# An expert loop placed at a fixed instruction slot, and GpSimd's attention work cut into four pieces a head

## The chip, the cores and the metric

The kernel runs on one core of a Trainium2 chip. The metric is the device time of one execution in microseconds. The engines are TensorE (PE; its weight loads are listed as PEld), VectorE (DVE), ScalarE (ACT), GpSimd (POOL) and SyncE (SP), which issues most DMAs. Each has its own instruction stream; they meet through semaphores.

## The reference

Two layers (DEPTH) over 512 tokens of width 1024, in float32:

```
h = rmsnorm(x);  proj = h @ w_in
ya = chunk attention, 8 heads, key band of 9 chunks of 64, learned relative bias
yb = sliding-window attention, 8 heads on 2 kv heads, window 128, ALiBi and sinks
x += (sigmoid(gate0) * (ya @ w_a) + sigmoid(gate1) * (yb @ w_b)) @ w_out
layer 0:  x += (silu(h @ w_gate) * (h @ w_up)) @ w_down        # dense, 2816 wide
layer 1:  x += sum over top 2 of 8 experts, softmax weight * swiglu_e(h), 1408 wide
out = rmsnorm(x)
```

## The kernel before, in words

All large products are made at float32 accuracy out of fp32r parts: each weight unit (128x1024) is loaded by SP into `raw`, ACT copies its high part (`split_hi`, L642) and the low part is the difference (L929 on DVE, L480 on GpSimd), and PE multiplies hi·hi, hi·lo and lo·hi. Two split buffers and four raw buffers go round.

**Attention of a layer.** There are 16 heads: 0 to 7 belong to the first mixer (chunk attention, bias from `rel_ext`), 8 to 15 to the second (ALiBi). A head has four steps, one for each block of 128 queries, so a layer has 64. PE, ACT and DVE run a loop of ticks written out by hand (L1467, L738, L1022). A step's scores go to PSUM; DVE adds the bias and takes the maximum (L1032, L1040), ACT takes the exponential, DVE takes the reciprocal and multiplies the probabilities by it (L1049, called the normalisation here, which raises `probs_ready`); two ticks after the scores PE transposes them (L1491, with the bias tile's turning at L1447 in a head's first step) and later multiplies by the values. Between these PE works off one gate unit (L1336 to L1338) every four ticks: gate g is used in ticks 4g to 4g+3.

GpSimd's part (L506 to L528): for each head of the first mixer it issues a DMA of bias rows (L512), masks a corner (L515), makes the low part of a gate unit (`gate_lo`, L480: 1024 columns, as soon as ACT's high part is there), and splits a finished head's output into high (`head_split`, L500) and low part (L502) as soon as DVE has raised `y_added`; for heads of the second mixer it makes the ALiBi tile and its sink column (`distance_tile`, L490, L492).

**Experts.** A loop of eight passes, one for each expert, runs on SP, ACT, DVE and PE (`passes`, L853 on ACT, L1252 on DVE, L1639 on PE). A pass has 35 weight units: 24 gate and up units in three chunks (512, 512 and 384 columns), 11 down units. SP loads seven ahead (`m_raw`), ACT and DVE split five ahead (`m_hi` L839, `m_lo` L1238). Each pass begins with five instructions that load the expert's token count and branch: with more than 128 tokens it runs the Then body (two slots, 128 and 64 rows), else the Else body (one slot). At its end ACT copies the result (`y_stage` L892, and L895 with two slots), and the next pass begins with the load of the activation table (L861). A second loop of the same code, for experts with more than 192 tokens, follows and is skipped. With these inputs experts 0, 1, 6 and 7 take the Then body, 2 to 5 the Else body.

Of the kernel before, what the change touches and what calls it, by code (L numbers as in the profile page):

```python
# [5 lines left out]
F32 = mybir.dt.float32  # L6
# [4 lines left out]
ALU = mybir.AluOpType  # L11
# [3 lines left out]
P = 128  # L15
D = 1024
T = 512
DEPTH = 2
# [40 lines left out]
ROUNDS = -(-T // CAP)  # L59
LISTS = ROUNDS * EXPERTS * SLOTS  # L60
PAD_H, PAD_Y = T, 2 * T


def build_kernel(nc, xT, g_mix, w_in, b_gate, rel_ext, sinks, w_a, w_b, w_out, g_ffn, w_gu, w_down, w_router,
                 moe_gu, moe_down, g_ffn_row, g_final_row, out):
    ctx = ExitStack()
    with ctx:
# [242 lines left out]
        def split_of(n, c0, c1):  # L310

            return w_hi[:, n % SPL, c0:c1], w_lo[:, n % SPL, c0:c1]
# [126 lines left out]
        def _(pool):  # L439
# [27 lines left out]
            def double_keys(layer):  # L467
                for u in K_UNITS:
                    pool.wait_ge(drained_dve, layer * N_PROJ + u + 1)
                    for own, hi, lo, other in halves(u):  # L470
                        pool.dma_start(hi[other, :], hi[own, :]).then_inc(k_doubled, 16)
                        pool.dma_start(lo[other, :], lo[own, :]).then_inc(k_doubled, 16)

            def gate_lo(layer, g):

                n = MIX_START[layer] + U_GATE + g + 2
                hi, lo = split_of(n, 0, UNIT)
                pool.wait_ge(hi_ready, n + 1)
                pool.wait_ge(lo_ready, n)
                pool.tensor_tensor(lo, raw[:, n % RAW, :], hi.bitcast(F32), ALU.subtract).then_inc(lo_ready, 1)  # L480
                pool.wait_ge(lo_ready, n + 1)

            def distance_tile(layer, hh):

                H = layer * 2 * HEADS + hh
                head = step(TT * hh)["head"]
                if hh == HEADS:
                    pool.wait_ge(consts, 4)
                pool.wait_ge(nmax_ready, TT * (H - 1))
                pool.tensor_scalar(bias_t[:, H % 2, 2 * P:T], alibi[:], -2.0 ** -(head + 1), None, ALU.mult)  # L490
                pool.wait_ge(bias_ready, H)
                pool.tensor_copy(bias_t[:, H % 2, T:T + 1], sink[:, layer, head:head + 1]).then_inc(bias_ready, 1)  # L492

            def head_split(layer, hh):

                H = layer * 2 * HEADS + hh
                r = step(4 * hh)["rows"]
                y_hi, y_lo = y_tiles(hh)
                pool.wait_ge(y_added, H + 1)
                pool.tensor_copy(y_hi[r:r + HD, :], y_sum[r:r + HD, :]).then_inc(y_hi_ready, 1)  # L500
                pool.wait_ge(y_hi_ready, H + 1)
                pool.tensor_tensor(y_lo[r:r + HD, :], y_sum[r:r + HD, :], y_hi[r:r + HD, :].bitcast(F32),  # L502
                                   ALU.subtract).then_inc(y_lo_ready, 1)
                pool.wait_ge(y_lo_ready, H + 1)

            for i in range(DEPTH * HEADS):  # L506

                if i % HEADS:
                    pool.wait_ge(bias_turned, i)
                else:  # L510
                    pool.wait_ge(rinv_spread, 2 * (i // HEADS) + 1)
                pool.dma_start(bias[:], bass.AP(tensor=rel_ext.tensor, offset=i * 384, ap=[[1, P], [1, 2 * P]])).then_inc(bias_in, 16)  # L512
                pool.wait_ge(bias_in, 16 * (i + 1))

                pool.memset(bias[HD:P, 3 * HD:4 * HD], MASKED).then_inc(bias_masked, 1)  # L515
                if i % HEADS == 0:
                    double_keys(i // HEADS)
                pool.wait_ge(bias_masked, i + 1)
                if i % HEADS >= 2:
                    gate_lo(i // HEADS, i % HEADS - 2)  # L520
                if i % HEADS >= 3:
                    head_split(i // HEADS, i % HEADS - 3)
                if i % HEADS == HEADS - 1:
                    for j in range(HEADS - 2, 2 * HEADS):
                        gate_lo(i // HEADS, j)
                        head_split(i // HEADS, j - 1)
                        if j + 2 < 2 * HEADS:
                            distance_tile(i // HEADS, j + 2)  # L528
            steps = [0]

            def one(ins):
# [103 lines left out]
        def _(act_):  # L635
# [215 lines left out]
            turned_x(0, 1)  # L851

            def passes(first, sections, always_both):  # L853
                with A.Fori(0, sections) as i:
                    def pass_of(slots):

                        def moved(half, of):
                            A.activation(m_other[:, half, 0:of.shape[1]], of, ACT.Copy).then_inc(tail_moved, 1)


                        A.activation(warm[:], eps[:], ACT.Silu)  # L861
                        for u in range(M_UNITS):
                            A.wait_ge(m_done, i * M_UNITS + (first * M_UNITS + u + 1))
                            v = u + M_SPL
                            expert_hi(i * (16 * (M_UNITS // M_RAW)) + 16 * (first * (M_UNITS // M_RAW) + v // M_RAW + 1), v)
                            for c in range(len(CHUNKS)):
                                w = CHUNKS[c] * P
                                if u == CHUNK_END[c]["gate"]:
                                    if slots > 1:
                                        if c == 0:  # L870
                                            A.wait_ge(y_copied, i * SLOTS + (SLOTS * first + SLOTS))
                                        moved(0, ps[TAIL:P, 1, 0:w])
                                    A.wait_ge(m_act_ready, i * 6 + (6 * first + 2 * c + 1))
                                    A.activation(m_silu[:, 0, 0:w], ps[:, 0, 0:w], ACT.Silu).then_inc(m_silu_ready, SLOTS // slots)
                                    if slots > 1:
                                        A.wait_ge(tail_summed, i * len(CHUNKS) + (len(CHUNKS) * first + c + 1))
                                        A.activation(m_silu[0:TAIL, 1, 0:w], m_silu[0:TAIL, 1, 0:w], ACT.Silu).then_inc(m_silu_ready, 1)
                                if u == CHUNK_END[c]["up"] and slots > 1:
                                    A.wait_ge(m_act_ready, i * 6 + (6 * first + 2 * c + 2))
                                    moved(1, ps[TAIL:P, 3, 0:w])  # L880
                            if u in TURNED_AT:
                                c = TURNED_AT[u]
                                nb = CHUNKS[c]
                                for sl in range(slots):
                                    A.wait_ge(at_turned, i * 6 + (6 * first + SLOTS + 2 * c + sl + 1))
                                    A.activation(parts_of(at_hi, at_lo, at_both, sl, 4 * c, 4 * c + nb)[0],
                                                 used_columns(ps[:, 4 + sl, 0:nb * P].rearrange("p (k c) -> p k c", c=P), sl),
                                                 ACT.Copy).then_inc(at_hi_ready, SLOTS // slots)
                            if u in TURN_X:
                                turned_x(i * 4 + 4 * (first + 1), TURN_X.index(u))  # L890
                        A.wait_ge(stage_free, i * SLOTS + (SLOTS * first + 1))
                        A.activation(y_stage[:, 0, :], ps[:, Y_BANKS[0]:Y_BANKS[0] + 2, :].rearrange("p b c -> p (b c)"),  # L892
                                     ACT.Copy).then_inc(y_copied, SLOTS // slots)
                        if slots > 1:
                            A.activation(m_other[:].rearrange("p b c -> p (b c)"),  # L895
                                         ps[TAIL:P, Y_BANKS[1]:Y_BANKS[1] + 2, :].rearrange("p b c -> p (b c)"),
                                         ACT.Copy).then_inc(tail_moved, 1)
                        else:
                            A.sem_inc(tail_moved, T_MOVES)

                    if always_both:
                        pass_of(SLOTS)
                    else:
                        with A.If(A.value_load(counts[0:1, bass.ds(i, 1)], min_val=0, max_val=T) > P):
                            pass_of(SLOTS)
                        with A.Else():
                            pass_of(1)
# [17 lines left out]
        def _(V):  # L925
# [324 lines left out]
            turned_x(0, 1)  # L1250

            def passes(first, sections, always_both):  # L1252
                with V.Fori(0, sections) as i:
                    def pass_of(slots):

                        moves0 = T_MOVES * first
# [524 lines left out]
```

## Time and profile before

| | us |
|---|---|
| median of 3 runs | 1744.6 (1744.45 to 1745.5) |
| the profiled execution's own time | 1746.57 |
| its span, first to last instruction | 1744.5 |
| PE busy | 1610.8 (92%) |
| DVE busy | 1070.3 (61%) |
| ACT busy | 851.0 (49%) |
| POOL busy | 249.8 (14%) |

The mean granted TensorE clock is 0.969. The profile comes from one execution. Busy shares are means over stages that differ: attention takes about 123 to 285 us and 842 to 1005 us, the expert passes about 1137 to 1711 us. A granted clock (PEclk) of 1.00 is 2.4 GHz, 0.50 is 1.2 GHz. Idle time of an engine that nothing waits for costs nothing.

### The profile page before, as it was taken

The numbers are of one execution on the slowest core, as the hardware profiler recorded it, in microseconds if no ns is written. First come the engines' busy times: TensorE is split into PE (matmuls) and PEld (weight loads), VectorE is DVE, ScalarE is ACT, GpSimd is POOL, SyncE is SP. The second block draws the span as 40 slices with busy tenths as digits, with TensorE's granted clock in tenths as the row PEclk, the third lists the DMA queues.
The fourth block names the chain that finished last, engine by engine and source line by source line (L and its number), as shares of the span: only waits on it lengthen the run. The fifth ranks groups of instructions, "written<-read, shape, count | busy, mean of one in ns | idle before, by whom it ended". The sixth has DMA issues, their size and how long they took to land.

```text
span 1744.5 us, 22792 instructions
## 1 busy us (share of the span) xinstructions
PE 1610.8 (92%) x7630; PEld 1328.9 (76%) x7631; DVE 1070.3 (61%) x1671; ACT 851.0 (49%) x1312; POOL 249.8 (14%) x272
## 2 busy tenths in 40 slices
PE   8999999999999999999999999699997879799991
PEld 6877777788888888888777787488886668688881
DVE  6647776654444433365577756656567668676665
ACT  5436664343333322243566634455556667675653
POOL 2004453000000000020245500400000110110002
PEclk9999999999999999999999999899999899899996
DMA  7332111223333233353221121657677789796764
GB/s 201 113 96 61 52 61 61 97 97 97 97 97 97 94 92 95 106 143 104 70 58 49 61 86 60 229 165 238 196 241 273 287 307 332 268 329 224 223 217 181
DMA packets 79143, 259.74 MB, mean 149 GB/s; under 512 B 12384, under 2 KB 12384, under 8 KB 78512
## 3 DMA queue, kind: packets, MB, share of 16 engines
q1 hardware_dynamic: 71056, 239.16, 41.6%
q0 software_dynamic: 7968, 19.21, 4.0%
q8 instruction: 48, 0.79, 0.2%
q14 instruction: 71, 0.58, 0.1%
HBM read 244.70 MB, written 9.47 MB: 146 GB/s over the span
## 4 chain that ended last, share of the span: by engine, by line
PE 81%; DVE 10%; issue 4%; ACT 2%; DMA 1%; ACTq 0%; POOL 0%; SPq 0%; POOLq 0%; PEldq 0%; DVEq 0%
PE ps L1336 16%; PE ps L1338 15%; PE ps L1337 15%; PE ps L1648 7%; PE ps L1650 6%; PE ps L1649 6%; PE ps L1646 3%; PE ps L1647 3%; DVE probs L1049 3%; PE ps L1491 2%; PE ps L1629 1%; PE ps L1504 1%; PE ps L1503 1%; PE ps L1524 1%; PE ps L1523 1%
## 5 line engine op out<-in xcount | busy, mean ns | idle before, releaser
L1238 DVE TENSOR_TENSOR m_lo<-m_raw,m_hi 128x1024 fp32r<-128x1024 f32 (+1 forms) x285 | 324.8, 1162 | 156.2 <-ACT m_hi L839 152.7
L1336 PE MATMUL ps<-h_hi,w_hi 128*128 128x512 f32 x904 | 362.4, 401 | 4.5 <-DVE w_lo L929 2.7
L839 ACT ACTIVATE m_hi<-m_raw 128x1024 fp32r<-128x1024 f32 (+1 forms) x285 | 283.4, 1009 | 162.4 <-PE ps L1647 121.3
L1337 PE MATMUL ps<-h_lo,w_hi 128*128 128x512 f32 x904 | 354.7, 392 | 0.0
L1338 PE MATMUL ps<-h_hi,w_lo 128*128 128x512 f32 x904 | 354.4, 392 | 0.0
L642 ACT ACTIVATE w_hi<-raw 128x1024 fp32r<-128x1024 f32 (+1 forms) x169 | 177.0, 1048 | 350.3 <-PE ps L1338 347.0
L929 DVE TENSOR_TENSOR w_lo<-raw,w_hi 128x1024 fp32r<-128x1024 f32 x137 | 165.7, 1209 | 147.5 <-ACT w_hi L642 147.3
L1338 PEld LDWEIGHTS ps<-h_hi,w_lo 128*128 128x128 f32 x904 | 170.7, 189 | 37.1
L1336 PEld LDWEIGHTS ps<-h_hi,w_hi 128*128 128x128 f32 x904 | 171.1, 189 | 32.5 <-DVE w_lo L929 3.1
L1337 PEld LDWEIGHTS ps<-h_lo,w_hi 128*128 128x128 f32 x904 | 171.4, 190 | 26.8 <-issue 0.7
L1648 PE MATMUL ps<-m_hi,xt_hi 128*128 128x512 f32 (+1 forms) x384 | 149.6, 390 | 40.2 <-DVE m_lo L1238 38.3
L1649 PE MATMUL ps<-m_lo,xt_hi 128*128 128x512 f32 (+1 forms) x384 | 146.4, 381 | 0.0
L1650 PE MATMUL ps<-m_hi,xt_lo 128*128 128x512 f32 (+1 forms) x384 | 146.2, 381 | 0.0
L1648 PEld LDWEIGHTS ps<-m_hi,xt_hi 128*128 128x128 f32 x384 | 74.8, 195 | 55.4 <-DVE m_lo L1238 41.3
L588 POOL DMA_INDIRECT xg<-h_dram,lists x20 | 26.7, 1334 | 505.1 <-PE ps L1629 363.2
L1049 DVE TENSOR_SCALAR probs<-probs,stat 128x256 f32<-128x256 f32 (+3 forms) x128 | 93.3, 729 | 5.0
L480 POOL TENSOR_TENSOR w_lo<-raw,w_hi 128x1024 fp32r<-128x1024 f32 x32 | 76.4, 2387 | 82.8 <-ACT w_hi L642 45.7
L512 POOL DMA_DIRECT2D norm<-rel_ext x16 | 9.3, 579 | 542.8 <-PE ps L1363 479.4
L1649 PEld LDWEIGHTS ps<-m_lo,xt_hi 128*128 128x128 f32 x384 | 75.0, 195 | 10.7
L1650 PEld LDWEIGHTS ps<-m_hi,xt_lo 128*128 128x128 f32 x384 | 74.5, 194 | 11.2
L747 ACT ACTIVATE pT_hi<-ps 128x256 fp32r<-128x256 f32 (+3 forms) x128 | 50.6, 395 | 58.2 <-PE ps L1491 56.4
L1648 PE MATMUL ps<-m_hi,at_hi 128*128 128x512 f32 x176 | 70.8, 402 | 1.6 <-PEq L1662 1.6
(244 smaller groups left out, 2900.9 us busy)
## 6 DMA issues: line engine op xcount, KB each, us to landing
m_raw<-moe_g SPq DMA_DIRECT2D x135, 512.0 KB, 4.9
m_raw<-moe_down SPq DMA_DIRECT2D x88, 512.0 KB, 5.0
raw<-w_in SPq DMA_DIRECT2D x68, 512.0 KB, 3.5
m_raw<-moe_g SPq DMA_DIRECT2D x64, 384.0 KB, 3.8
raw<-w_gu SPq DMA_DIRECT2D x44, 512.0 KB, 3.5
raw<-w_out SPq DMA_DIRECT2D x16, 512.0 KB, 3.5
raw<-w_down SPq DMA_DIRECT2D x16, 512.0 KB, 3.6
raw<-w_a SPq DMA_DIRECT2D x8, 512.0 KB, 3.5
```

What stands on the lines that cost most here:

```text
L480: pool.tensor_tensor(lo, raw[:, n % RAW, :], hi.bitcast(F32), ALU.subtract).then_inc(lo_ready, 1)
L642: A.activation(split_of(n, 0, cols)[0], raw[:, n % RAW, 0:cols], ACT.Copy).then_inc(hi_ready, 1)
L839: A.activation(m_hi[:, u % M_SPL, 0:cols], m_raw[:, u % M_RAW, 0:cols], ACT.Copy).then_inc(m_hi_ready, 1)
L929: V.tensor_tensor(lo, raw[:, n % RAW, 0:cols], hi.bitcast(F32), ALU.subtract).then_inc(lo_ready, 1)
L1049: V.tensor_scalar(t[:, 0:nk], t[:, 0:nk], stat[:, 5, c:c + 1], None, ALU.mult).then_inc(probs_ready, 1)
L1238: V.tensor_tensor(m_lo[:, u % M_SPL, 0:cols], m_raw[:, u % M_RAW, 0:cols], m_hi[:, u % M_SPL, 0:cols].bitcast(F32), ALU.subtract).then_inc ...
L1336: E.matmul(ps[:, bank, :], wh, hi, start=first, stop=False)
L1337: E.matmul(ps[:, bank, :], wh, lo, start=False, stop=False)
L1338: return E.matmul(ps[:, bank, :], wl, hi, start=False, stop=final)
L1648: E.matmul(out, hi[:, x, :], wh, start=start, stop=False)
L1649: E.matmul(out, hi[:, x, :], wl, start=False, stop=False)
L1650: return E.matmul(out, lo[:, x, :], wh, start=False, stop=stop)
```

## The change

Two parts. On ACT and DVE the expert loop is built with a loop head placed at instruction slot 16 of a fetch block; this goes for both loops that `passes` makes, and the padding ahead of a head is branched over. On GpSimd, the low part of a gate unit is made in two halves of 512 columns, the head's split is taken apart into `head_hi` and `head_lo`, and a wait (`after_step`) for the end of one step's normalisation stands ahead of each of the four: steps 4·hh+8 to 4·hh+11 in the turn of head hh. The bias rows' DMA, its mask and the ALiBi tile are put between them.

```diff
+LOOP_SLOT = 16
+            def after_step(layer, s):
+                pool.wait_ge(probs_ready, layer * STEPS + min(s, STEPS - 1) + 1)
-            def gate_lo(layer, g):
+            def gate_lo(layer, g, half):
                 n = MIX_START[layer] + U_GATE + g + 2
+                c0, c1 = half * UNIT // 2, (half + 1) * UNIT // 2
+                hi, lo = split_of(n, c0, c1)
+                if half == 0:
+                    pool.wait_ge(hi_ready, n + 1)
+                    pool.wait_ge(lo_ready, n)
+                ins = pool.tensor_tensor(lo, raw[:, n % RAW, c0:c1], hi.bitcast(F32), ALU.subtract)
+                if half == 1:
+                    ins.then_inc(lo_ready, 1)
+                    pool.wait_ge(lo_ready, n + 1)
...
-            for i in range(DEPTH * HEADS):
-                (bias rows, mask, gate_lo, head_split, distance_tile one after the other)
+            for layer in range(DEPTH):
+                bias_rows(layer * HEADS)
+                bias_mask(layer * HEADS)
+                double_keys(layer)
+                bias_rows(layer * HEADS + 1)
+                bias_mask(layer * HEADS + 1)
+                for hh in range(-2, 2 * HEADS - 1):
+                    if hh >= -1:
+                        after_step(layer, 4 * hh + 8)
+                        gate_lo(layer, hh + 1, 0)
+                        after_step(layer, 4 * hh + 9)
+                        gate_lo(layer, hh + 1, 1)
+                    if hh + 4 < HEADS:
+                        bias_rows(layer * HEADS + hh + 4)
+                    if hh >= 0:
+                        after_step(layer, 4 * hh + 10)
+                        head_hi(layer, hh)
+                    if hh + 4 < HEADS:
+                        bias_mask(layer * HEADS + hh + 4)
+                    elif hh + 4 < 2 * HEADS:
+                        distance_tile(layer, hh + 4)
+                    if hh >= 0:
+                        after_step(layer, 4 * hh + 11)
+                        head_lo(layer, hh)
...
-                with A.Fori(0, sections) as i:
+                with nc.Fori(0, sections, engines=[A.engine], head_slot={A.engine: LOOP_SLOT}) as i:
...
-                with V.Fori(0, sections) as i:
+                with nc.Fori(0, sections, engines=[V.engine], head_slot={V.engine: LOOP_SLOT}) as i:
```

## Rows read from the trace of the kernel before

**Rows 1.** The page, the chain that ended last: shares of the span by engine.

```profile
PE 81%; DVE 10%; issue 4%; ACT 2%; DMA 1%; ACTq 0%; POOL 0%; SPq 0%; POOLq 0%; PEldq 0%; DVEq 0%
```

**Rows 2.** Stretches: us, busy PE, PEld, DVE, ACT, POOL, PEclk, DMA share, GB/s.

```profile
122.60:210.00 87.40, 81.40 (x447) 66.37 (x446) 64.25 (x178) 52.54 (x128) 34.80 (x35) 0.99 0.19 54
...
1304.30:1364.60 60.30, 50.72 (x239) 42.54 (x238) 46.18 (x47) 42.10 (x50) 5.30 (x4) 0.94 0.81 290
...
1486.20:1548.10 61.90, 51.52 (x239) 43.13 (x238) 44.62 (x46) 41.11 (x49) 5.30 (x4) 0.92 0.85 302
```

**Rows 3.** Waits, 130 to 285 us: total us, times, longest.

```profile
PE ps L1491 <- DVE probs L1049: 8.1, 12, 1.0
...
PE ps L1447 <- DVE probs L1049: 3.3, 6, 0.6
```

**Rows 4.** Waits, 850 to 1003 us, the second of the two.

```profile
PE ps L1447 <- DVE probs L1049: 3.2, 6, 0.6
```

**Rows 5.** Timeline, 197 to 204 us: start, us, engine, line, idle before.

```profile
197.67 2.39 POOL L480 TENSOR_TENSOR w_lo<-raw,w_hi 128x1024 fp32r<-128x1024 f32 x1 [4.66 <-issue]
198.63 1.52 DVE L1049 TENSOR_SCALAR probs<-probs,stat 128x128 f32<-128x128 f32 x1
202.28 1.44 DVE L1049 TENSOR_SCALAR probs<-probs,stat 128x256 f32<-128x256 f32 x1
202.29 1.28 POOL L502 TENSOR_TENSOR q_both<-y_sum,q_both 64x512 fp32r<-64x512 f32 x1
```

**Rows 6.** Single lines over the span: duration ns min/median/max; L512's DMA.

```profile
L1049 DVE TENSOR_SCALAR probs<-probs,stat x128: 286/440/1660, 124.9 to 1000.7; 128x256 f32<-128x256 f32 x64, 128x128 f32<-128x128 f32 x32, 128x384 f32<-128x384 f32 x16, 128x512 f32<-128x512 f32 x16
...
L500 POOL CAST q_both<-y_sum x30: 602/610/614, 147.1 to 1005.4; 64x512 fp32r<-64x512 f32 x30
...
L490 POOL TENSOR_SCALAR bias_t<-alibi x16: 848/852/878, 203.7 to 990.5; 128x256 f32<-128x256 f32 x16
...
DMA to landing us min/median/max: 3.1/3.2/4.2
```

**Rows 7.** The chain that ended last, 1364 to 1380 us.

```profile
1364.63 1.01 ACT y_stage L892
1365.64 4.07 issue
...
1370.52 4.48 issue
```

**Rows 8.** Waits, 1300 to 1560 us: total us, times, longest.

```profile
DVE m_lo L1238 <- ACT m_hi L839: 70.2, 44, 12.5
ACT L861 <- issue: 41.9, 5, 10.4
...
PE ps L1648 <- DVE m_lo L1238: 35.9, 8, 9.3
...
ACT m_hi L839 <- DMA m_raw<-moe_down: 0.7, 1, 0.7
```

**Rows 9.** Timeline of PE, first products after two of the four waits.

```profile
1318.58 0.80 PE L1648 MATMUL ps<-m_hi,xt_hi 128*128 128x512 f32 x1 [8.53 <-DVE m_lo L1238]
...
1501.37 0.79 PE L1648 MATMUL ps<-m_hi,xt_hi 128*128 128x512 f32 x1 [9.34 <-DVE m_lo L1238]
```

**Rows 10.** Stretches after the last of the four waits and in a pass.

```profile
1496.00:1506.10 10.10, 4.73 (x11) 3.76 (x12) 6.01 (x6) 7.75 (x9) 0.00 (x0) 0.50 0.33 112
1321.80:1350.00 28.20, 27.54 (x137) 23.83 (x135) 25.45 (x27) 21.81 (x25) 0.00 (x0) 1.00 0.94 336
```

**Rows 11.** The chain: one product at the lower and one at the upper clock.

```profile
1319.80 0.43 PE ps L1650
...
1346.27 0.23 PE ps L1650
```

**Rows 12.** The page, DMA queues: packets, MB, share of 16 engines.

```profile
q14 instruction: 71, 0.58, 0.1%
```

More of the change, by code:

```diff
@@ L472, in double_keys, with bias_rows, bias_mask @@
                         pool.dma_start(lo[other, :], lo[own, :]).then_inc(k_doubled, 16)
-            def gate_lo(layer, g):
+            def after_step(layer, s):
+                pool.wait_ge(probs_ready, layer * STEPS + min(s, STEPS - 1) + 1)
+            def gate_lo(layer, g, half):
                 n = MIX_START[layer] + U_GATE + g + 2
[L477 to L481, printed above, removed]
+                c0, c1 = half * UNIT // 2, (half + 1) * UNIT // 2
[7 more added lines that the diff above has]
+                    pool.wait_ge(lo_ready, n + 1)
+            def bias_rows(i):
+                if i % HEADS:
+                    pool.wait_ge(bias_turned, i)
+                else:
+                    pool.wait_ge(rinv_spread, 2 * (i // HEADS) + 1)
+                pool.dma_start(bias[:], bass.AP(tensor=rel_ext.tensor, offset=i * 384, ap=[[1, P], [1, 2 * P]])).then_inc(bias_in, 16)
+            def bias_mask(i):
+                pool.wait_ge(bias_in, 16 * (i + 1))
+                pool.memset(bias[HD:P, 3 * HD:4 * HD], MASKED).then_inc(bias_masked, 1)
+                pool.wait_ge(bias_masked, i + 1)
             def distance_tile(layer, hh):
@@ L492, in distance_tile, with head_hi, head_lo @@
                 pool.tensor_copy(bias_t[:, H % 2, T:T + 1], sink[:, layer, head:head + 1]).then_inc(bias_ready, 1)
-            def head_split(layer, hh):
+                pool.wait_ge(bias_ready, H + 1)
+            def head_hi(layer, hh):
+                H = layer * 2 * HEADS + hh
+                r = step(4 * hh)["rows"]
+                pool.wait_ge(y_added, H + 1)
+                pool.tensor_copy(y_tiles(hh)[0][r:r + HD, :], y_sum[r:r + HD, :]).then_inc(y_hi_ready, 1)
+                pool.wait_ge(y_hi_ready, H + 1)
+            def head_lo(layer, hh):
                 H = layer * 2 * HEADS + hh
@@ L498, in head_split @@
                 y_hi, y_lo = y_tiles(hh)
-                pool.wait_ge(y_added, H + 1)
-                pool.tensor_copy(y_hi[r:r + HD, :], y_sum[r:r + HD, :]).then_inc(y_hi_ready, 1)
-                pool.wait_ge(y_hi_ready, H + 1)
                 pool.tensor_tensor(y_lo[r:r + HD, :], y_sum[r:r + HD, :], y_hi[r:r + HD, :].bitcast(F32),
@@ L504, in head_split @@
                 pool.wait_ge(y_lo_ready, H + 1)
-            for i in range(DEPTH * HEADS):
[L508 to L528, printed above, removed]
+            for layer in range(DEPTH):
[22 more added lines that the diff above has]
+                        head_lo(layer, hh)
             steps = [0]
```

## The prediction

> **What bounds the kernel now.** The chain that ended last is the first view to read: 81% of it is TensorE (PE), 10% VectorE (DVE) [rows 1]. So whatever doesn't open or close a wait of PE is worth nothing, and the reader looks for the places where PE stands. The table of stretches gives two kinds [rows 2]: attention (86 + 74 us per layer, PE busy some 93%) and the four passes over experts with at most 128 tokens (243.8 us in all: 60.3, 60.8, 60.8, 61.9, first and last shown), where PE is busy for only 51 us of each while the other four passes, over experts with more tokens, take some 80 us and keep PE full. The table of waits says what PE waits for in either.
>
> In attention it is the normalisation, L1049: 12 + 6 waits of 11.4 us in layer 0 [rows 3], 11.3 us in layer 1 (8.1 and 3.2 [rows 4]). Busy PE is modelled with 0.39 us for a 512-column product, although one follows another at 0.23 us [rows 11], so each wait costs 0.16 us more than the view says: 18 × 0.16 = 2.9 us. PE loses 14.3 us in layer 0, 14.2 in layer 1: 28.5 us. The timeline shows why [rows 5]: GpSimd (POOL) starts the gate split (L480, 2.39 us) at 197.67, DVE issues its 128x128 normalisation at 198.63, and that ends 0.08 us after GpSimd does, after 1.52 us; undisturbed it is 0.29 us [rows 6]. At 202.28 the same happens against L502. In each layer all 15 first steps of heads 1 to 15 are caught by L480, and three second steps by L502: 18, as many as there are waits.
>
> In the expert passes PE waits for m_lo at the start of a pass [rows 8, 9]: 8.53, 8.33, 7.96 and 9.34 us, with the 0.16 us each 34.8 us. Behind it is the scalar engine (ACT): after y_stage the chain holds 4.07 us in which ACT waits for nothing, five loop-head instructions, and another 4.48 us [rows 7]; before the table load at L861 it stood 41.9 us in five of the passes, 37.2 in these four [rows 8]. Those are its two taken branches, back to the loop head and on to the Else body. DVE runs the same two branches and its waits hold only ACT's work [rows 8]. After each standstill PE is granted 0.50, 1.2 GHz, for 6.8, 10.2, 10.2 and 10.2 us (the last stands in [rows 10]); it is busy 3.2, 4.5, 5.6 and 4.7 us of those, with a product every 0.43 us instead of 0.23 [rows 11], so 18.0 × 0.20 / 0.43 = 8.4 us. Together 43.2 us are lost in the four passes.
>
> **Part 1, the loop head (ACT, DVE).** Counted in the program, ACT's loop is 292 instructions (5 head, 149 Then, 136 Else, 2 end), DVE's 223. The instruction packets are 0.58 MB / 71 = 8.2 KB [rows 12], 128 instructions of 64 bytes. Set beside ACT's position in straight code, they come each time it is about 64 (mod 128) past the program's start. With these borders ACT's loop, at 1197, lies in four blocks, and its end stands in the last, where a fifth is asked for; DVE's, at 1464, lies in three and asks for a fourth. DVE never stands, ACT stands at both branches: I take it that four blocks are held and the fifth displaces the head, then the head's reload the Else. From slot 16 ACT's 292 end at 308: three blocks and one ahead, which is DVE's case now. DVE's end at 239, two blocks and one ahead: nothing to gain or lose.
>
> If both stalls go, ACT's idle time ahead of the table load falls from 9.4 us to 9.36 - 4.07 - 4.48 + 0.5 for two ordinary branches = 1.3 us (0.5 is my estimate; no row has them on ACT alone: between nothing and 4 us). ACT's four idle times shrink by 37.2 - 5.2 = 32.0 us, against 34.8 us that PE waits: some 3 us of waits stay (PE has five prepared weight units, 6.8 us of work, and y_stage 1.01, branches 1.3, table load 1.5, m_hi 1.06 and m_lo 1.24 take 6.1 from the last product; the first of the four adds m_other). Waits under a microsecond brought no half clock, so the 8.4 us go whole. The next thing that can be late is the weights. PE wants one every 1.36 (6 × 0.227). Where it is full the DMA share is 0.94 [rows 10] and in the four passes m_hi waited once for a DMA, 0.7 us [rows 8], so the loads hold this pace; row gathers and scatters, which now run while PE stands, will compete. I take 1 us for it. Part 1: 43.2 - 3 - 1 = 39.2 us. Bounds: 0 (nothing changes) and 43.2.
>
> Price of the placing: one taken branch over padding ahead of each loop. At the entry ACT has five units ready (PE needs over 10 us for them in a two-slot pass), and at the exit, where the second, skipped loop is padded too and the jump reaches further, about 10 us pass in moving rows out and in before the mix. A stall like the 4.1 or 4.5 us is hidden at both; were it not, 4 to 9 us. That Then-passes save 2 to 4 us on ACT at a back edge is worth nothing: PE waits for no m_lo there.
>
> **Part 2, GpSimd's pieces.** L480 becomes two of 512 columns: L502 does 512 in 1.28 [rows 5], so 2.56 for 2.39; both bounds are near (half of 2.39 is 1.20). The cast is 0.61, the ALiBi tile 0.85 and 0.18 [rows 6]. Each group now starts when a normalisation ends, and the next starts one step later. In the second mixer a head will take 9.33 - 0.85 = 8.5 us, 2.12 a step; less the normalisation's own 0.35, 1.77 us are free. First half 1.35 with its semaphore, second half 1.35, lo part 1.35: free of collisions. Cast with tile and sink column: 1.84, an overhang of 0.07. In the first mixer a step has 2.4 us.
>
> The waits added, and what is queued behind them: the second half of gate g waits for step 4g+5, and the bias rows' DMA, the cast, the mask and the lo part stand behind it. PE wants the unit in its step 4g+8. By the times of head 7 the half would be done at 202.28 + 0.35 + 1.35 = 203.98; the unit's first product is at 206.87, so 2.9 us spare. The bias DMA (3.2 us to landing, [rows 6]) is issued 1.6 us after the second step's normalisation and masked at +5.1; the lo part, behind it in GpSimd's queue, starts at +5.2 instead of +4.8 and ends at +6.5, just ahead of the next normalisation at +6.8. If a landing takes 4.2 us, as one did, that one collides: at most 1.2 us on DVE, 0.7 on PE, for four heads a layer. I take 1 us in all; bounds 0 and 6. The slack that turned 1.23 to 1.37 us of delay into 0.7 to 0.85 of waiting remains, so the 28.5 us go whole, less this: 27.5 us. SP's loads follow lo_ready, at most one step later, at a DMA share of 0.19: hidden. At the end of attention GpSimd's last pieces shift by 0.3 us and end before DVE's own last split.
>
> On the pair of memory ports which DVE and GpSimd share, the Trainium skill (SBUF — State Buffer, section SBUF: two separate sides) says that whoever starts first holds it for its whole instruction. The ends 0.08 us apart agree. By that rule a shorter piece that still collides costs up to its 1.28 us, which is the first rival below.
>
> **Sum.** 27.5 + 39.2 = 66.7 us. The profiled execution took 1746.57 us around a span of 1744.5, so 1679.9; the median of the runs lies 2.0 lower, 1744.6, giving **1678 us**.
>
> **Rivals.**
> - Collisions move: the four pieces begin close to a normalisation, because semaphores and steps are uneven, and one piece a head still catches one. For it: only 0.4 us are free behind each half, 0.2 behind some lo parts. Then attention gains 8 of 28 us: 1744.6 - 8 - 39 = 1698.
> - One of ACT's two stalls stays: the head's block is displaced by the block asked for ahead of the loop's end, and the Else is found. Then PE waits 4.2 to 4.8 us in four passes (17.8) and keeps 7 us of half clock, so part 1 gives 17.4: 1700. Against it: DVE's three blocks hold now. The Trainium skill (Runtime: NRT & Kernel Launch, Instruction fetch mechanics) gives this outcome: it has an engine hold just two lines of 16 KiB, 256 instructions, read on in sequence, and ACT's body from 16 to 308 would still cross a border. The 8.2 KB packets [rows 12] and DVE without a stall speak against that size.
> - Weights become the bound in the short passes: their DMA share of 0.81 to 0.85 is 202 us of full load [rows 2], and if 0.95 is the most that can be had, the four passes need 213 us, not 205: 1686.
> - The placing does nothing (both stalls stay): 1717.
> - Slower: GpSimd falls behind. A piece that misses its step's gap waits behind another's DMA, the second half ends over 2.9 us later than now, and PE stands a step, 2.3 us, for each of 32 gate units: 74 us, more than the 39 gained: 1744.6 + 74 - 39 = 1780. It decides from 2.9 us of lateness; GpSimd's work is 5.6 us a head plus 3.2 of waiting for DMA, of 8.5 to 10 us.
>
> **Numbers.** Forecast 0.62 (own range 1671 to 1684), weights 0.14, collisions 0.08, one stall 0.07, nothing from the placing 0.04, slower 0.03, smaller mixtures near no change 0.02. The range reaches over the weights' case and most of the collisions': 1670 to 1697. It leaves some 0.17 out. A measurement tells 0.2%, 3.5 us, from nothing: faster 0.95, within 0.02, slower 0.03.
>
> **What would show it.** L1049's longest falls from 1.66 to about 0.5 us, PE has hardly a wait left for it, and heads take 8.5 us (second mixer) and 10.0 (first). In the short passes PE's wait at the start is under 2 us, each lasts some 51 us, the granted clock stays at 1, and the 4 us pieces without a reason are gone from the chain. It is wrong if such a piece remains, if L1049 has many above 1 us, or if m_hi waits for DMAs.

## The result and the profile after

| | before | after |
|---|---|---|
| median, us | 1744.53 (1744.24 to 1745.5) | 1670.82 (1669.97 to 1671.59) |
| ratio, 95% interval | | 0.9576 (0.956 to 0.9593) |
| span of the profiled execution, us | 1744.5 | 1669.4 |

The kernel is 73.7 us faster (by the spans 75.1); 66.7 were forecast, to 1678 us, and the time lies in the range.

The page after: busy PE, the engines' shares of the chain [rows 1], and the instruction packets [rows 12].

```profile
PE 1590.5 (95%) x7630; PEld 1325.5 (79%) x7631; DVE 1024.3 (61%) x1671; ACT 852.5 (51%) x1312; POOL 257.5 (15%) x304
...
q14 instruction: 39, 0.32, 0.1%
...
PE 87%; DVE 6%; issue 2%; ACT 2%; DMA 1%; POOL 0%; ACTq 0%; SPq 0%; POOLq 0%; DVEq 0%; PEldq 0%
```

The stretches after, columns as in [rows 2]: the two halves of attention in layer 0, and the second, third and fourth of the four one-slot passes.

```profile
122.00:202.00 80.00, 80.00 (x448) 67.91 (x447) 53.45 (x181) 53.04 (x129) 36.31 (x43) 0.98 0.19 59
202.00:269.40 67.40, 67.40 (x394) 57.44 (x393) 45.63 (x173) 46.32 (x119) 43.37 (x46) 1.00 0.21 64
...
1322.90:1372.90 50.00, 48.95 (x238) 41.57 (x237) 44.23 (x46) 40.90 (x49) 5.30 (x4) 1.00 0.98 365
1372.90:1423.00 50.10, 49.05 (x239) 41.65 (x238) 44.33 (x46) 41.11 (x50) 5.31 (x4) 1.00 0.98 370
1423.00:1473.00 50.00, 48.95 (x239) 41.48 (x238) 44.26 (x45) 40.87 (x49) 5.30 (x4) 1.00 0.99 371
```

Attention, from a layer's first normalisation to its last, takes 141.2 and 140.5 us instead of 156.2 and 156.2: 30.7 less. The four passes take 200.5 instead of 243.8: 43.3 less. PE is busy through both stretches of attention, and the granted clock is 1.00 in all four passes; the other stages differ by a microsecond or so either way.

The waits in attention of layer 0 after (130 to 270 us; total, times, longest). PE itself has none left for the normalisation, now L1079; two of its weight loads have one [rows 3]. The first row is new and free: GpSimd waits by design.

```profile
POOL w_lo L487 <- DVE probs L1079: 29.2, 30, 4.0
...
PEld ps L1521 <- DVE probs L1079: 0.4, 1, 0.4
PEld ps L1477 <- DVE probs L1079: 0.3, 1, 0.3
```

One head of the second mixer on the timeline (start, us; compare [rows 5]): each GpSimd piece starts about 0.1 us behind a normalisation and ends before the next; only the sink column's 0.18 us runs 0.07 us into one. A head lasts 235.60 - 227.20 = 8.40 us, before 9.32.

```profile
227.20 0.29 DVE L1079 TENSOR_SCALAR probs<-probs,stat 128x128 f32<-128x128 f32 x1
227.62 1.29 POOL L487 TENSOR_TENSOR w_lo<-raw,w_hi 128x512 fp32r<-128x512 f32 x1 [0.90 <-DVE probs L1079]
229.16 0.35 DVE L1079 TENSOR_SCALAR probs<-probs,stat 128x256 f32<-128x256 f32 x1
229.59 1.29 POOL L487 TENSOR_TENSOR w_lo<-raw,w_hi 128x512 fp32r<-128x512 f32 x1 [0.67 <-DVE probs L1079]
231.23 0.35 DVE L1079 TENSOR_SCALAR probs<-probs,stat 128x256 f32<-128x256 f32 x1
231.72 0.61 POOL L523 CAST q_both<-y_sum 64x512 fp32r<-64x512 f32 x1 [0.84 <-DVE stat L1070]
232.42 0.85 POOL L513 TENSOR_SCALAR bias_t<-alibi 128x256 f32<-128x256 f32 x1
233.22 0.18 POOL L515 COPY bias_t<-sink 128x1 f32<-128x1 f32 x1
233.33 0.35 DVE L1079 TENSOR_SCALAR probs<-probs,stat 128x256 f32<-128x256 f32 x1
233.83 1.30 POOL L531 TENSOR_TENSOR q_both<-y_sum,q_both 64x512 fp32r<-64x512 f32 x1 [0.43 <-DVE probs L1079]
235.60 0.29 DVE L1079 TENSOR_SCALAR probs<-probs,stat 128x128 f32<-128x128 f32 x1
```

ACT between two one-slot passes (timeline; compare [rows 7]): the table load follows y_stage without a gap.

```profile
1322.91 1.01 ACT L922 ACTIVATE y_stage<-ps 128x1024 f32<-128x1024 f32 x1
1323.94 1.28 ACT L891 ACT_TABLE_LOAD   x1
```

And what PE and ACT wait for from 1265 to 1480 us [rows 8]. Of PE's 35.9 us 2.2 are left, in waits 15 and 26 us into a pass, most of which stood there before; at the start of a pass PE now waits 0.08 us once and otherwise not at all. ACT now waits for DMAs.

```profile
ACT m_hi L869 <- DMA m_raw<-moe_g: 6.1, 18, 0.8
...
PE ps L1678 <- DVE m_lo L1268: 2.2, 6, 0.4
```

### The profile page after: what moved, and what is told of

Read it like the earlier page. It is cut to its first block, busy times and chain, and to the rows that moved or that the text cites. A ratio compares the mean times of both kernels' runs of the same rounds, so it can differ in the third digit from the quotient of the medians.

```text
span 1669.4 us, 22896 instructions
## 1 busy us (share of the span) xinstructions
PE 1590.5 (95%) x7630; PEld 1325.5 (79%) x7631; DVE 1024.3 (61%) x1671; ACT 852.5 (51%) x1312; POOL 257.5 (15%) x304
## 3 DMA queue, kind: packets, MB, share of 16 engines
q1 hardware_dynamic: 71056, 239.16, 43.3%
## 4 chain that ended last, share of the span: by engine, by line
PE 87%; DVE 6%; issue 2%; ACT 2%; DMA 1%; POOL 0%; ACTq 0%; SPq 0%; POOLq 0%; DVEq 0%; PEldq 0%
PE ps L1366 18%; PE ps L1368 17%; PE ps L1367 17%; PE ps L1678 6%; PE ps L1680 6%; PE ps L1679 6%; PE ps L1676 4%; PE ps L1677 4%; PE ps L1521 2%; PE ps L1554 1%; DVE m_lo L1268 1%; PE ps L1534 1%; PE ps L1659 1%; PE ps L1553 1%; PE ps L1533 1%
## 5 line engine op out<-in xcount | busy, mean ns | idle before, releaser
L1367 PEld LDWEIGHTS ps<-h_lo,w_hi 128*128 128x128 f32 x904 | 171.4, 190 | 26.8 <-issue 0.7
L1678 PE MATMUL ps<-m_hi,xt_hi 128*128 128x512 f32 (+1 forms) x384 | 145.2, 378 | 6.5 <-DVE m_lo L1268 4.9
L487 POOL TENSOR_TENSOR w_lo<-raw,w_hi 128x512 fp32r<-128x512 f32 x64 | 82.5, 1291 | 59.2 <-DVE probs L1079 58.5
L1677 PE MATMUL ps<-m_lo,xt_both 128*128 128x512 f32 (+1 forms) x192 | 71.7, 373 | 0.0
L1676 PE MATMUL ps<-m_hi,xt_both 128*128 128x512 f32 (+1 forms) x192 | 71.7, 373 | 0.0
```

Source lines behind the costliest of these rows:

```text
L1367: E.matmul(ps[:, bank, :], wh, lo, start=False, stop=False)
L1676: E.matmul(out, both[:, x, :], wh, start=start, stop=False)
L1677: return E.matmul(out, both[:, x, :], wl, start=False, stop=stop)
L1678: E.matmul(out, hi[:, x, :], wh, start=start, stop=False)
```

## The experiments

Times are medians. There are three groups: e1 to e4, e5 to e8, and e9 to e12. Each group ran on one chip with the kernel before beside it (1747.46, 1746.76 and 1746.15 us), so between groups the ratios to it are compared.

**e1: the loops alone, and e2: GpSimd alone.** e1 is the kernel before with this edit, e2 the changed kernel without it:

```diff
-                with A.Fori(0, sections) as i:
+                with nc.Fori(0, sections, engines=[A.engine], head_slot={A.engine: LOOP_SLOT}) as i:
-                with V.Fori(0, sections) as i:
+                with nc.Fori(0, sections, engines=[V.engine], head_slot={V.engine: LOOP_SLOT}) as i:
```

> The kernel before with the ACT and DVE expert loops placed at slot 16; GpSimd's attention work as before. Theory (the parts are independent): 44 to 45 us come from the expert passes (43.3 us from the four one-slot passes, 1.3 from the second pass), so about 1700 us, ratio 0.974. Rival (the new GpSimd program also shifts or relieves something in the expert stage): a gain under 40 us here, and the missing part only in the full change.

> The changed kernel with both expert loops unplaced. Theory: attention alone gives 30 to 31 us (15.0 in layer 0, 15.7 in layer 1), so 1714 us; the one-slot passes stay at 60 to 62 us with PE waits of 8 to 9 us. Rival: removing the attention waits also changes the loop's position or the clock, so that the sum of the two parts misses 73.7 us by over 3 us.

Measured: e1 1703.25 us, ratio 0.9755 (0.9732 to 0.9777), 44 us less than before; its four passes take 200.99 us. e2 1715.40 us, ratio 0.9821 (0.9804 to 0.9838), 32 us less; its passes still take 59 to 62 us. The product of the two ratios is 0.9580, the full change has 0.9576. The parts are independent, and the passes' gain is all the loop's.

**e3, e4, e12: other slots for ACT's loop.** One number is changed (DVE's stays 16):

```diff
-                with nc.Fori(0, sections, engines=[A.engine], head_slot={A.engine: LOOP_SLOT}) as i:
+                with nc.Fori(0, sections, engines=[A.engine], head_slot={A.engine: 104}) as i:
```

> The changed kernel with ACT's loop head at slot 104 and DVE's at 16. ACT's 291 instructions then end at 395 and lie in four blocks of 128, with a fifth asked for ahead. Theory A (four blocks are held and a miss starts the reading anew): both branches stall as in the kernel before, one-slot passes of 60 us, about 1714 us. Theory B (only the displaced head block is missing, the Else is still held): one stall, some 1692 us. Rival (any placing helps, because the stall came from something else): 1671 us.

> The changed kernel with ACT's loop head at slot 80: it ends at 371, in three blocks of 128, one ahead. Theory: as slot 16, 1671 us, no stall at L891 (the table load). Rival (blocks of 256 instructions, two held: 80 to 371 crosses one border just as 16 to 307 does, but slot 104 would too): 80 and 104 behave alike.

> The changed kernel with ACT's loop head at slot 96: its last two instructions are at 385 and 386, 1 and 2 past the border of the fourth block, where slot 80 stops at 371 and slot 104 at 394. Theory (the fifth block is asked for as soon as the fourth is entered): both branches stall in each one-slot pass, as at 104, some 1715 to 1720 us. Rival (the limit is not a border between 80 and 104 but the number of instructions beyond it, or lies past 387): 1671 us.

Measured, with two runs each: slot 104 1722.24 us (ratio 0.9861), slot 96 1721.82 us (1716.94 and 1726.70, ratio 0.9866), slot 80 1673.53 us (0.9582). At 104 both stalls are there, between two one-slot passes (the chain):

```profile
1335.91 1.01 ACT y_stage L922
1336.92 3.27 issue
...
1341.42 5.00 issue
```

How long ACT stood ahead of the table load in all eight passes, slot 104:

```profile
issue: 58.9, 8
```

and slot 80:

```profile
issue: 1.0, 1
```

Slot 96, where only the last three or four instructions are past the border at 384, has 59.2 us in eight. (The expectations count 291 instructions where the prediction has 292; nothing hangs on that one.) The instruction packets number 76 at 104 and at 96, 39 at 80, 71 in the kernel before. The kernel before reads four of them around one stall, from 1363 to 1377 us:

```profile
q14 instruction: 4, 0.03, 0.8%
```

The changed kernel reads none from 1323 to 1473 us, in three whole passes. So it is the position and no other effect of placing a loop, the step lies between 80 and 96, and theory A is right about the stalls: a loop that needs one block too many pays at both branches. Its time of 1714 us was 8 us too low. A badly chosen slot is worse than none: the two-slot passes, which had hidden their stall at the old position, take up to 82.1 us (slot 104) and 85.0 (slot 96, in the slower of its two runs) instead of 79.9, and the four one-slot passes 247 and 246 instead of 243.8.

**e5 and e10: the pieces without their waits; e11: the changed kernel beside e10.**

```diff
             def after_step(layer, s):
-                pool.wait_ge(probs_ready, layer * STEPS + min(s, STEPS - 1) + 1)
+                return
```

> The changed kernel without the four after_step waits: the same pieces in the same order, each as early as its data allow. Theory (the waits place the pieces between normalisations): the first half starts about 1 us ahead of a head's first normalisation as before and now holds it for some 0.3 us, and the second half follows at once and holds it for 1.3 us more, so most of the gain is lost: attention 15 to 28 us longer, 1686 to 1699 us. Rival (cutting the 2.39 us piece in two is what helps, since DVE gets in between the halves): within 4 us of the changed kernel.

> The changed kernel without the four waits once more, beside the changed kernel itself on one chip. Theory (the cut does it, the waits are worth the held 0.3 us that PE's slack takes): within 0.1% of the changed kernel. Rival (the waits are worth some 3 us, as the medians of different chips suggest): 0.2% longer.

> The changed kernel, unaltered, as the reference for the run without the waits: ratio 0.9576 to the kernel before, as measured.

Measured: e5 1676.74 us, ratio 0.9594 (0.9578 to 0.961). My theory of 15 to 28 us more is wrong and its rival right. Side by side on one chip, e10 has 1674.48 us, 0.9592 (0.9578 to 0.9606), and the changed kernel 1671.50, 0.9581 (0.9567 to 0.9595). That is 0.18% more, which is nearer to e10's rival (0.2%) than to its theory (0.1%), but the intervals overlap, so the time alone decides nothing. Attention takes 141.0 and 141.6 us in the profiled execution of e10, 141.0 and 140.7 in that of e11, so the waits are worth about 1 us there. Another 2.4 us between these two executions are in the second expert pass (85.55 against 83.15 us), where PE's first jump back is followed by 3.4 us at half clock in some profiled executions and not in others. It doesn't go with the waits: slot 80 and e6, which have them, show it, and e9, which has none, doesn't. Why the cut alone does it, e5's timeline of GpSimd shows first:

```profile
219.19 2.54 POOL L487 TENSOR_TENSOR w_lo<-raw,w_hi 128x512 fp32r<-128x512 f32 x2 [0.94 <-POOL q_both L531]
```

and that of DVE:

```profile
219.96 0.61 DVE L1079 TENSOR_SCALAR probs<-probs,stat 128x128 f32<-128x128 f32 x1
```

The normalisation starts in the first half's time, is held for 0.3 us, and ends in the middle of GpSimd's 2.54 us: DVE gets in between the halves. Holding it for 0.3 us costs PE next to nothing: a head of the second mixer takes 8.41 us in e5, 8.40 in the changed kernel.

**e6: one piece with the wait.** The changed kernel with the gate's low part whole again:

```diff
-                c0, c1 = half * UNIT // 2, (half + 1) * UNIT // 2
+                c0, c1 = 0, UNIT
...
                         after_step(layer, 4 * hh + 8)
-                        gate_lo(layer, hh + 1, 0)
-                        after_step(layer, 4 * hh + 9)
                         gate_lo(layer, hh + 1, 1)
```

> The changed kernel with the gate's low part in one piece of 1024 columns (2.39 us), started after the first step's normalisation; the other waits stay. Theory (a piece must fit between two normalisations): in the first mixer 2.4 us are free, no loss; in the second the next normalisation comes after 1.67 us and is held for 0.7 us, of which PE's slack of 0.5 us takes most: 0 to 5 us longer than the changed kernel, 1671 to 1676 us. Rival (the cut is needed): over 10 us longer.

Measured: 1675.68 us, ratio 0.9589 (0.9573 to 0.9605). As expected: heads of the first mixer take 9.75 us as in the changed kernel, those of the second 8.66 instead of 8.40. There the piece of 2.40 us starts just behind one normalisation and runs into the next, first GpSimd:

```profile
220.35 2.40 POOL L488 TENSOR_TENSOR w_lo<-raw,w_hi 128x1024 fp32r<-128x1024 f32 x1 [0.89 <-DVE probs L1078]
```

then DVE:

```profile
221.90 1.01 DVE L1078 TENSOR_SCALAR probs<-probs,stat 128x256 f32<-128x256 f32 x1
```

That normalisation is held for 0.65 us (1.01 instead of 0.35), and the head is 0.26 us longer: so PE has some 0.4 us of slack (my estimate, the difference). Attention takes 142.5 and 142.8 us, 3.6 us more than in the changed kernel.

**e9: neither cut nor wait.** e6's edit and e5's together, so that only the new order is left.

> The changed kernel with the gate's low part in one piece and without the after_step waits: only the new order of GpSimd's work is left of part 2 (with the head's split in two calls). Theory (either the cut or the wait is enough, and one of them is needed): the first normalisation of a head is held for 1.2 to 1.4 us again, attention as in the kernel before but for the three second steps a layer that the new order may free: 24 to 30 us above the changed kernel, 1695 to 1701 us. Rival (the new order alone brings the gain, and neither cut nor wait matters): 1671 to 1676 us.

Measured: 1698.30 us, ratio 0.9731 (0.9716 to 0.9746), 26.8 us above the changed kernel on the same chip. The waits are back in layer 0 (130 to 285 us):

```profile
PE ps L1520 <- DVE probs L1078: 6.1, 9, 0.7
PE ps L1476 <- DVE probs L1078: 3.3, 6, 0.6
```

They are the 15 first steps; the three second steps, 3 × 0.7 us a layer, are freed by the order. This closes the square: cut and wait 0.9581, cut alone 0.9592, wait alone 0.9589, neither 0.9731.

**e7: the normalisation reads PSUM.** The kernel before, GpSimd untouched; in the first mixer ACT writes its exponentials back to PSUM, where DVE reads them.

```diff
-                            A.activation(probs[:, s % 2, 0:st["nk"]], ps[:, S_BANK + s % 2, 0:st["nk"]], ACT.Exp, scale=-1.0,
+                            A.activation(ps[:, S_BANK + s % 2, 0:st["nk"]], ps[:, S_BANK + s % 2, 0:st["nk"]], ACT.Exp, scale=-1.0,
...
-                        V.tensor_scalar(t[:, 0:nk], t[:, 0:nk], stat[:, 5, c:c + 1], None, ALU.mult).then_inc(probs_ready, 1)
+                        if st["a"] and s >= 2:
+                            V.wait_ge(pT_ready, s - 1)
+                        src = ps[:, S_BANK + s % 2, 0:nk] if st["a"] else t[:, 0:nk]
+                        V.tensor_scalar(t[:, 0:nk], src, stat[:, 5, c:c + 1], None, ALU.mult).then_inc(probs_ready, 1)
```

> The kernel before, but in the first mixer ACT leaves the exponentials in PSUM and DVE's normalisation reads them there (SBUF is only written). GpSimd's work is as before. Theory (what is held is the SBUF to SBUF form of the operation, not DVE as a whole): the 1.5 us normalisations of heads 1 to 7 fall to 0.3 to 0.7 us, PE's ten waits a layer there go, 13 to 15 us in all, 1730 to 1732 us. Rival (any DVE work is held while GpSimd runs, and the normalisation only happens to be next): they stay at 1.5 us, no gain or a loss, 1744 us or more.

Measured: 1730.08 us, ratio 0.99 (0.9884 to 0.9917), 16.7 us less, a little more than expected. DVE's groups in layer 0 (times | busy us, mean ns of one | idle):

```profile
L1052 DVE TENSOR_SCALAR probs<-probs,stat 128x128 f32<-128x128 f32 x8 | 13.0, 1628 | 0.3
...
L1052 DVE TENSOR_SCALAR probs<-ps,stat 128x128 f32<-128x128 f32 x8 | 2.8, 350 | 0.3
```

Out of PSUM the first step's normalisation takes 350 ns on the mean although GpSimd runs beside it; out of SBUF, in the second mixer of the same execution, 1628. In both layers together, 14 of these normalisations start 0.97 to 0.99 us into GpSimd's 2.39 us and end over 1 us ahead of it. Heads 1 to 6 take 9.80 us, and those of the second mixer still 9.3. It is this form of the operation that is held, not DVE.

**e8: PE's loop placed too**, by the same edit as e1's on `E.Fori`.

> The changed kernel with PE's expert loop placed at slot 16 too. The only wait of PE at a back edge is the first, 3.15 us between products at 1188 us, with no half clock after it. Theory (it is PE's jump over the Else body, read for the first time, whatever the position): unchanged, 1671 us within 0.2%. Rival (the position of PE's loop causes it): 2 to 3 us faster.

Measured: 1672.66 us, ratio 0.9582 (0.956 to 0.9605): no change, though its runs spread from 1669.3 to 1678.1, too far to tell the rival's 2 to 3 us from nothing. The trace decides: the wait at the first jump back stays (2.4 us; 2.8 in the changed kernel and 2.4 in e9, where PE's loop isn't placed).

```profile
1190.56 0.49 PE L1678 MATMUL ps<-m_hi,xt_hi 128*128 128x512 f32 x1 [2.44 <-DVE m_lo L1268]
```

## Why the prediction was right, point by point

- **What bounds the kernel:** right in both places. Both kinds of waits went, and with them 74 us. (The first stretch of attention is 87.4 us in [rows 2], where the prediction writes 86; no sum uses it.)
- **Part 1, that four blocks of 128 are held and the fifth displaces the head:** borne out by slots 80, 96 and 104, by the packets (71, now 39), and by both stalls coming together. What exactly is thrown away on a miss wasn't tried. The Trainium skill's two lines of 256 instructions (Runtime: NRT & Kernel Launch, Instruction fetch mechanics) would leave a stall at slot 16 and not tell 80 from 96, as from either slot the loop crosses one border of 256. ACT has no stall at 16, and 80 and 96 differ, so the measurements decide against it here.
- **Part 1, the size:** 43.3 us came in the four passes, 39.2 were forecast. The mis-sized term is what was kept back: 3 us of waits and 1 us for DMA. At the start of the four passes PE waits 0.08 us in all. The waits were worked out with 1.3 us between y_stage and the table load (0.5 of it for ordinary branches, the rest for the five head instructions). Measured it is 0.02 us (1322.91 + 1.01 to 1323.94): the chain shows them executed by ACT's sequencer while y_stage still runs. And m_hi waits 6.1 us in 18 pieces for DMAs, but it is prepared five units ahead, so PE hardly sees it.
- **The weights' rival:** wrong. It took 0.95 for the most of the DMA share; the last three of the four passes run at 0.98 to 0.99, 365 to 371 GB/s, with PE full. It was near, though: little room is left.
- **The price of placing:** nothing, as forecast. Entry and end of the loop take the same time. From the last y_stage to the end both e1 and the kernel before take 36.5 us, and ahead of the first pass PE waits 9.8 and 1.0 us in e1, 9.7 and 1.0 in the kernel before.
- **Part 2, the mechanism:** right that the held normalisation makes PE wait. That only its form out of SBUF is held the prediction didn't say; e7 shows it. Sized at 27.5 us, measured 30.7; heads take 8.40 us where 8.5 was forecast, and 9.75 where it was 10.0. The 1 us kept back for collisions wasn't needed: one lo part was met (1 of 128 normalisations at 0.86 us, the longest). Another 2 us go beyond the 28.5 us of waits; PE's time around a wait is slightly longer than the 0.16 us allowed, which is argued from the sum, not shown.
- **Part 2, what does it:** here a step failed, though not one of the sum. "Each group now starts when a normalisation ends" was taken for the cause. e5, e6 and e9 show that the cut alone gives all but about 1 us of it, and the wait alone all but 4 us. I wrote in e5's expectation that the second half would follow at once and hold DVE again; in fact DVE, which has been waiting, comes in between.
- **Collisions move, GpSimd falls behind:** neither. PE never waits for a low part that GpSimd makes, so the second half is in time.

## What to carry to other kernels

Where two engines exclude each other, cut the long operation of the one that isn't critical: the critical one gets in between the pieces and waits for what is left of one piece, which a few tenths of slack absorb; timing the pieces is a second, smaller step. Read such a case from pairs of ends that agree to 0.1 us. For a loop on one engine, count its instructions and where they lie: a body with If and Else that touches one fetch block too many pays several microseconds at the jump back and again at the jump to Else, and code changed anywhere ahead of it moves it there. The value of a stall is what the bottleneck lost by it, the lower clock after it too.

## What the runs showed of the hardware that was not expected

- Instructions of ACT come in packets of 8.2 KB. That a packet is 128 instructions was worked out ahead of the runs, and the step between slots 80 and 96 fits it. Between two one-slot passes a taken branch out of what is held left ACT idle for 3.3 to 5.9 us (kernel before, slots 96 and 104), though a packet itself takes 0.32 us at the median and 1.4 at most.
- A branch within what is held cost ACT nothing between two passes: loop end, loop head, the load of a count and the jump to Else ran beside a 1.01 us operation.
- A normalisation out of PSUM (128x128: 0.35 us) is slower than one out of SBUF (0.29) when nothing disturbs either, and the faster beside a busy GpSimd: 0.35 against 1.5 to 1.6 us.
- PE's first jump back in the expert loop leaves it without a product for 2.7 to 4.2 us in the nine profiled executions in which ACT's loop doesn't stall (2.8 in e8, with PE's loop placed, and 2.8 in the kernel before). Five of them (e1, e4, e5, e6, e10) have 3.4 us at half clock after it and a second pass of 85.1 to 85.7 us; four (the changed kernel, e8, e9, e11) have none and 82.6 to 83.2 us. The later jumps back show nothing of the kind. Why is open; a difference of 2.5 us between two kernels can be this alone.
